# A decode-and-prompt step on one core: two of the next eight weight blocks asked for in front of the SP queue's wait for the samples' vectors

## The chip, the cores and the metric

The kernel runs on one core of one Trainium2 chip. The metric is the device time of one launch in microseconds (us); less is better. The core has five engines, each with its own instruction queue: PE (matmul), ACT (activations and copies out of PSUM), DVE (vector work), POOL, and SP, which here issues nearly all large transfers. A queue runs in order: an instruction that waits for a semaphore holds everything behind it on the same engine. A transfer, once issued, runs by itself and adds 16 to a semaphore when it has landed.

## The reference

Two layers of a hybrid decoder run for a prompt of 256 tokens and for 8 samples of one token each, with shared weights and 1024 channels. All is float32.

```python
xn   = rms_norm(x, ln1_g)
proj = xn @ w_in                    # four mixers' columns, then 4 x 1024 gate columns
y_a, y_b, y_c, y_d = rwkv7(...), hgrn2(...), retention(...), mlstm(...)
gates  = sigmoid(proj[..., o4:]).reshape(B, T, 4, 1024)
branch = einsum('btmw,mwd->btmd', ys, w_branch)
x = x + (sum over m of gates * branch) @ w_out
x = x + peer_ffn(rms_norm(x, ln2_g))      # 16 experts of 16384 for each of 8 heads
```

Each mixer keeps a state of 64 x 64 per head. For the samples that state is read, updated with one token's vectors, and read out again. The states, the last projected row ("shift") and the last rows before a convolution are outputs too.

## The kernel before, in words

Channels lie on the 128 partitions; the 264 columns of a tile are 256 prompt tokens and 8 samples. The two layers are written out one after the other. In a layer come the projections of the mixers (32 column tiles), the mixers, the samples' states, the gates, the branch projection, the output projection, and the experts (the longest part).

**Weight blocks and slots.** The dense weights lie in memory as 44 blocks a layer, each 128 x 2048 floats (1 MB). A block holds two column tiles. `ring` has four slots. `block_of(j, n)` on SP waits until slot j is free (semaphore `w_free[j]`, cleared by `take`), then issues the transfer of block n, which raises `w_full[j]` when it has landed. Blocks 0 to 15 are the mixers' columns, 16 to 31 the gates', 32 to 35 the branches', 36 to 39 the output projection's, 40 to 43 the queries'. PE takes `w_full[j]` before the first of a block's two tiles; ACT (for the gates) signals `w_free[j]` after it has copied the second out of PSUM. The first tile of a block goes to one PSUM bank and the second to another (banks 2 and 3 from tile 14 on), and PE takes `bank_free` of the bank before it writes it; ACT gives it back after its copy.

**Gate tiles as filling.** There are 32 gate tiles, each 8 matmuls of 128 x 264 and one copy by ACT. They depend on nothing but `xn` and their weights, so PE's program puts them between steps of the mixers, in numbers fixed by hand: `EARLY_GATES = 14` of them before the samples' states, then `GATES_AT = (4, 5, 2, 1)` at four places, and the last six before the branches. Gate tile g reads block 16 + g // 2 from slot (g // 2) mod 4. So tiles 14 and 15 read block 23 (slot 3), tiles 16 and 17 block 24 (slot 0), tiles 18 and 19 block 25 (slot 1), 20 and 21 block 26 (slot 2), 22 and 23 block 27 (slot 3).

**The samples' vectors.** PE turns 18 vectors of the samples (L838, L839), ACT copies them out (L1250, L1251, step `act_svt`), SP writes them to a scratch in memory (L452, L453), waits for that, and reads them back in another layout into `gv` and `gvv` (L455, L458). DVE waits for these, then works on the states, L1735 to L1760. Its L1736 raises `dve_sa`; PE sums that over partitions (L844), and DVE needs the sum at L1744. DVE's L1760 raises `dve_po`; PE needs it at L848 and L849, and DVE works on the outcome up to L1773, which PE waits for at L855.

PE's order around this, with the gate tiles (L620) in it:

```python
                gate_tiles(GATES_AT[0])                       # tiles 14 to 17
                close_banks(7)
                e.wait_ge(S("dve_sa"), 1)
                mm(bank(7, HD), C("quads"), sa, start=True, stop=True).then_inc(S("pe_step"), 1)
                gate_tiles(GATES_AT[1])                       # tiles 18 to 22
                e.wait_ge(S("dve_po"), 1)
                ...
                gate_tiles(GATES_AT[2])                       # tiles 23 and 24
                e.wait_ge(S("dve_yy"), 1)
```

ACT, right after its copies for `act_svt`, runs six activations over gates and outputs (L1253 to L1258), and only then copies tiles 14 and 15 out (L1152).

**SP's order before.** Blocks 20 to 23 are issued as their slots come free. Then SP waits for `act_svt`, issues the two writes, waits for them, issues the five reads, waits for `dve_shift` (long raised by then) and issues the output of the shift rows. Then come blocks 24 to 31, in a loop of two rounds of four, and after it the blocks of the branches and of the output projection.

Of the kernel before, what the change touches and what calls it, by code (L numbers as in the profile page):

```python
# [38 lines left out]
N_IN, N_MIXED = 32, 16  # L39
N_BLOCKS = N_IN + 4 + 4 + 4  # L40
# [125 lines left out]
def build(nc, A, O):  # L166

    with ExitStack() as ctx:
# [200 lines left out]
        def S(name):  # L369
            return once[name] if name in once else sems[name]  # L370
# [13 lines left out]
        def step(name):  # L384

            steps = PE_STEPS if name.startswith("pe_") else ACT_STEPS
            return steps.index(name.split("_")[1]) + 1

        def take(e, s, n):

            e.wait_ge(s, n)
            e.sem_clear(s)
# [30 lines left out]
        def _(e):  # L423
            e.dma_start(const[:, 0:FIRST], A["const"][:, 0:FIRST]).then_inc(S("sp_once"), 16)
            e.dma_start(x[:, :, :], A["x"]).then_inc(S("sp_once"), 16)
            for l in range(L):
# [5 lines left out]
                def block_of(j, n):  # L432

                    take(e, w_free[j], 1)
                    e.dma_start(ring[:, j, :], A["w"][bass.ds(n, 1)].rearrange("a p c -> p (a c)")).then_inc(w_full[j], 16)
# [12 lines left out]
                for j in range(4):  # L448
                    block_of(j, l * N_BLOCKS + N_MIXED + 4 + j)

                e.wait_ge(S("act_step"), step("act_svt"))
                e.dma_start(O["scratch"][0:NGLA * NS, :], svt[0:NGLA * NS, :, :].rearrange("p a b -> p (a b)")).then_inc(S("sp_svw"), 16)  # L452
                e.dma_start(O["scratch"][NGLA * NS:NVEC * NS, :], svt2[0:(NVEC - NGLA) * NS, :, :].rearrange("p a b -> p (a b)")).then_inc(S("sp_svw"), 16)  # L453
# [5 lines left out]

                e.wait_ge(S("dve_shift"), 1)  # L460
                e.dma_start(O["shift"][bass.ds(l, 1)].rearrange("a p c -> p (a c)"), out_shift[:, :, :].rearrange("p a b -> p (a b)")).then_inc(S("sp_out"), 16)
                with e.Fori(2, 4) as i:
                    for j in range(4):
                        block_of(j, l * N_BLOCKS + N_MIXED + i * 4 + j)
                for j in range(4):
                    block_of(j, l * N_BLOCKS + N_IN + j)
                for j in range(4):
# [1684 lines left out]
```

## Time and profile before

| | |
|---|---|
| median of 3 runs | 2277.74 us (2268.29 to 2278.77) |
| the profiled execution, its own time | 2278.82 us |
| its span, first to last instruction | 2276.7 us |
| PE busy | 2048.0 us, 90% |
| DVE busy | 1435.7 us, 63% |
| ACT busy | 829.7 us, 36% |
| mean granted TensorE clock | 0.961 |

The profile is one execution. Times are microseconds from the start of its span. PEld is the weight load of a matmul, which overlaps with PE's matmuls. The granted clock is 1.00 at 2.4 GHz and 0.50 at 1.2 GHz; a number between is a stretch in which both occur. In a row of the timeline the bracket at the end is the idle time of the engine before the row, and what ended it; "remote" there means a release that the profile can't name, such as a transfer's landing. Consecutive instructions of one line are merged in one row.

### The profile page before, as it was taken

How to read it: one execution, taken by the hardware profiler on the slowest of the kernel's cores; microseconds unless marked ns; L12 is line 12 of the kernel's file. 1: busy time of each engine (PE TensorE's matmuls, PEld its weight loads, DVE VectorE, ACT ScalarE, POOL GpSimd, SP SyncE). 2: the span in 40 equal slices, each digit the busy share in tenths (PEclk: the TensorE clock that was granted, in tenths of full speed). 3: DMA queues.
4: the chain of work that ended last, by engine and by line, in shares of the span. 5: the costliest groups of instructions: out<-in, count | busy, mean ns of one | idle time of the engine just before them, and what ended most of it. 6: DMA issues, size and time to landing. Idle time of an engine off the chain costs nothing.

```text
span 2276.7 us, 37176 instructions
## 1 busy us (share of the span) xinstructions
PE 2048.0 (90%) x13044; PEld 1253.7 (55%) x13044; DVE 1435.7 (63%) x3297; ACT 829.7 (36%) x2404; POOL 753.9 (33%) x658
## 2 busy tenths in 40 slices
PE   6999989989999777999889898899899997789996
PEld 5777768764444222555477776787544442235553
DVE  1425464559999898544623454754699989974445
ACT  1221222034445675333322213220444457743333
POOL 0400000025545567444403000000354557754452
PEclk9999889999999999999989999999999999999998
DMA  6330233559999999999853201434799999999996
GB/s 254 122 113 2 78 123 128 186 176 384 375 366 400 367 384 374 369 382 398 345 213 111 94 21 61 156 132 165 259 365 384 386 361 348 375 367 393 378 361 246
DMA packets 120670, 597.81 MB, mean 263 GB/s; under 512 B 38635, under 2 KB 40587, under 8 KB 57227
## 3 DMA queue, kind: packets, MB, share of 16 engines
q0 software_dynamic: 76032, 417.87, 47.4%
q1 hardware_dynamic: 42784, 174.46, 21.1%
q10 hardware_dynamic: 1696, 3.45, 0.4%
q8 instruction: 89, 1.46, 0.3%
q14 instruction: 69, 0.57, 0.1%
HBM read 724.97 MB, written 6.58 MB: 321 GB/s over the span
## 4 chain that ended last, share of the span: by engine, by line
PE 57%; DVE 18%; DMA 12%; issue 7%; ACT 3%; POOL 1%; another core or an unknown queue 1%; SPq 0%; DVEq 0%; POOLq 0%; ACTq 0%
PE ps L945 11%; PE ps L1012 11%; PE ps L557 10%; DMA arena<-in_uv,arena 7%; PE ps L620 7%; DMA ring<-in_uv,arena 4%; DVE arena L1933 4%; PE ps L971 3%; PE ps L908 3%; PE ps L877 3%; PE ps L891 3%; DVE arena L1835 1%; DVE arena L1834 1%; DVE arena L1831 1%
## 5 line engine op out<-in xcount | busy, mean ns | idle before, releaser
L1416 POOL DMA_INDIRECT arena<-in_uv,arena x264 | 340.1, 1288 | 298.9 <-PE ps L945 250.7
L1416 POOL DMA_INDIRECT ring<-in_uv,arena x264 | 328.8, 1246 | 290.2 <-PE ps L945 251.4
L1933 DVE SCALAR_TENSOR_TENSOR arena<-ring,arena 128x1024 bf16<-128x1024 f32 x264 | 320.4, 1225 | 134.5 <-DMA ring<-in_uv,arena 124.1
L1933 DVE SCALAR_TENSOR_TENSOR arena<-arena 128x1024 bf16<-128x1024 f32 x264 | 320.9, 1225 | 128.1 <-DMA arena<-in_uv,arena 117.3
L945 PE MATMUL ps<-arena 64*64 64x512 f32 x2112 | 295.5, 631 | 67.1 <-ACT arena L1309 66.9
L945 PE MATMUL ps<-ring,arena 64*64 64x512 f32 x2112 | 293.2, 630 | 56.0 <-ACT arena L1309 53.9
L1307 ACT ACTIVATE arena<-arena 128x1 f32<-128x1 f32 x528 | 106.5, 202 | 574.7 <-DVE arena L1933 573.8
L1406 POOL COPY arena<-arena 128x8 uint32 (+1 forms) x66 | 34.6, 525 | 740.7 <-DVEq L1907 740.3
L971 PEld LDWEIGHTS ps<-xn,ub 128*128 128x128 f32 x1024 | 181.5, 192 | 176.3 <-issue 159.1
L971 PE MATMUL ps<-xn,ub 128*128 128x256 f32 x1024 | 277.4, 404 | 0.0
L1012 PE MATMUL ps<-hold,ub 128*128 128x256 f32 x1024 | 265.8, 398 | 0.0
L1012 PEld LDWEIGHTS ps<-hold,ub 128*128 128x128 f32 x1024 | 182.7, 191 | 150.6 <-issue 132.0
L620 PE MATMUL ps<-xn,ring 128*128 128x264 f32 x1024 | 245.1, 398 | 14.5 <-remote 12.1
L557 PE MATMUL ps<-xn,ring 128*128 128x264 f32 x1024 | 241.1, 396 | 14.5 <-ACTq L1100 10.5
L557 PEld LDWEIGHTS ps<-xn,ring 128*128 128x128 f32 x1024 | 199.4, 196 | 54.1 <-issue 15.7
L620 PEld LDWEIGHTS ps<-xn,ring 128*128 128x128 f32 x1024 | 197.4, 195 | 51.7 <-issue 17.0
L1309 ACT ACTIVATE arena<-const,arena 128x64 f32<-128x64 f32 x528 | 184.3, 349 | 17.2
L1308 ACT ACTIVATE arena<-arena 128x1 f32<-128x1 f32 x528 | 155.6, 295 | 17.2
L945 PEld LDWEIGHTS ps<-arena 64*64 64x64 f32 x2112 | 56.4, 133 | 164.1 <-issue 164.1
L945 PEld LDWEIGHTS ps<-ring,arena 64*64 64x64 f32 x2112 | 57.4, 134 | 141.2 <-issue 140.9
L1105 ACT ACTIVATE arena<-ps 128x264 f32<-128x264 f32 x64 | 25.2, 394 | 233.8 <-PE ps L557 233.7
L1152 ACT ACTIVATE arena<-ps 128x264 f32<-128x264 f32 x50 | 19.3, 389 | 201.7 <-PE ps L620 201.3
(427 smaller groups left out, 2264.7 us busy)
## 6 DMA issues: line engine op xcount, KB each, us to landing
ring<-in_w SPq DMA_DIRECT2D x88, 1024.0 KB, 4.9
ub<-in_ud SPq DMA_DIRECT2D x64, 512.0 KB, 7.6
ub<-in_uv SPq DMA_DIRECT2D x64, 512.0 KB, 7.7
ring<-in_uv,arena POOLq DMA_INDIRECT x264, 11.0
arena<-in_uv,arena POOLq DMA_INDIRECT x264, 11.6
hold<-in_st SPq DMA_DIRECT2D x2, 2048.0 KB
out_st<-hold SPq DMA_DIRECT2D x2, 2048.0 KB
const<-in_const ACTq DMA_DIRECT2D x1, 2723.0 KB, 13.5
```

The costliest lines, as they stand in the source:

```text
L557: m = mm(bank(b), ring[:, j, at:at + P], xn[:, kt, :], start=kt == 0, stop=kt == KT - 1)
L620: m = mm(bank(b), ring[:, j, at:at + P], xn[:, kt, :], start=kt == 0, stop=kt == KT - 1)
L877: m = mm(bank(b), ring[:, j, at:at + P], yy[:, 2 * m_ + k, :], start=k == 0, stop=k == 1)
L891: m = mm(bank(6 + o % 2), ring[:, j, at:at + P], src[:, kt, :], start=kt == 0, stop=kt == KT - 1)
L945: m = mm(ps[chunk(q ^ half), SUM_BANK[tt] + half, :], dg[chunk(q), k, :], row(k)[chunk(q), D + 512 * half:D + 512 * half + 512], start=Fal ...
L971: m = mm(bank(4 + j % 4, SEQ), ub[:, j % UB, kt * P:kt * P + P], xn[:, kt, 0:SEQ], start=kt == 0, stop=kt == KT - 1)
L1012: m = mm(bank(4 + dt // 2, SEQ, SEQ * (dt % 2)), ub[:, j % UB, dt * P:dt * P + P], hd[:, j, :], start=False, stop=False, skip_group_check= ...
L1307: own(act(hge[:, k:k + 1], hid[:, k:k + 1], ACT.Gelu))
L1308: own(act(hgg[:, k:k + 1], hge[:, k:k + 1], ACT.Copy, scale=gate))
L1309: act(dg[:, k, :], C("channel"), ACT.Copy, scale=hgg[:, k:k + 1]).then_inc(dg_full[k], 1)
L1416: e.indirect_dma_start(out=row(k), out_offset=None, in_=A["uv"], in_offset=bass.IndirectOffsetOnAxis(ap=ix[:, par, k:k + 1], axis=0), **sk ...
L1933: stt(prod[:, n % 2, :], u, 1.0, xtok[:, tt, :], ALU.mult, ALU.mult, accum_out=hid[:, k:k + 1]).then_inc(S("dve_hid"), 1)
```

## The change

Blocks 24 and 25 are asked for in front of SP's wait for `act_svt`, right behind block 23. Blocks 26 to 31 stay behind the output of the shift rows, and are written out one by one in place of the loop. The slots are the same as before, and so is the order of the blocks among themselves. Nothing changes on PE, ACT, DVE or POOL.

```diff
                 for j in range(4):
                     block_of(j, l * N_BLOCKS + N_MIXED + 4 + j)
 
+                for j in range(2):
+                    block_of(j, l * N_BLOCKS + N_MIXED + 8 + j)
                 e.wait_ge(S("act_step"), step("act_svt"))
...
                 e.wait_ge(S("dve_shift"), 1)
                 e.dma_start(O["shift"][bass.ds(l, 1)].rearrange("a p c -> p (a c)"), out_shift[:, :, :].rearrange("p a b -> p (a b)")).then_inc(S("sp_out"), 16)
-                with e.Fori(2, 4) as i:
-                    for j in range(4):
-                        block_of(j, l * N_BLOCKS + N_MIXED + i * 4 + j)
+                for n in range(2, 8):
+                    block_of(n % 4, l * N_BLOCKS + N_MIXED + 8 + n)
```

## Rows read from the trace of the kernel before

**Rows 1.** The page: its first line, and busy time, share and instructions by engine.

```profile
span 2276.7 us, 37176 instructions
PE 2048.0 (90%) x13044; PEld 1253.7 (55%) x13044; DVE 1435.7 (63%) x3297; ACT 829.7 (36%) x2404; POOL 753.9 (33%) x658
```

**Rows 2.** Windows by stage: layer 0's mixers and projections, layer 0's experts.

```profile
core 0: us, PE busy (x) PEld busy (x) DVE busy (x) ACT busy (x) POOL busy (x), PEclk, DMA share, GB/s
0.00:442.00 442.00, 393.66 (x2510) 322.44 (x2510) 191.59 (x411) 91.69 (x183) 25.24 (x34) 0.95 0.34 122
442.00:1140.00 698.00, 630.16 (x3994) 303.23 (x3994) 522.29 (x1232) 322.16 (x1017) 347.04 (x297) 0.97 0.92 357
```

**Rows 3.** Timeline of SP, layer 0, 225 to 400 us: issues of transfers.

```profile
start us, us, engine line op out<-in xcount [idle before <-releaser]
234.62 26.60 SPq L435 DMA_DIRECT2D ring<-in_w  x4
...
302.42 1.38 SPq L453 DMA_DIRECT2D scratch<-arena  x1
...
309.71 89.92 SPq L435 DMA_DIRECT2D ring<-in_w  x14
```

**Rows 4.** Timeline of ACT: tiles 9, 11, 14 and 15 in layer 0; 14 and 15 in layer 1.

```profile
269.61 0.37 ACT L1152 ACTIVATE hold<-ps 128x264 f32<-128x264 f32 x1
...
275.02 0.39 ACT L1152 ACTIVATE hold<-ps 128x264 f32<-128x264 f32 x1 [3.17 <-PE ps L620]
...
309.71 0.65 ACT L1152 ACTIVATE arena<-ps 128x264 f32<-128x264 f32 x2
...
1433.17 0.65 ACT L1152 ACTIVATE arena<-ps 128x264 f32<-128x264 f32 x2
```

**Rows 5.** Timeline of PE and DVE around the samples' states, layer 0.

```profile
301.17 7.29 PE L620 MATMUL ps<-xn,ring 128*128 128x264 f32 x32
...
311.46 1.87 DVE L1736 TENSOR_REDUCE arena<-arena 128x64 f32<-128x1024 f32 x1
...
315.10 10.24 PE L620 MATMUL ps<-xn,ring 128*128 128x264 f32 x32 [6.64 <-remote]
...
321.16 3.36 DVE L1742 TENSOR_TENSOR hold<-hold,arena 128x3072 f32<-128x3072 f32 x1
...
325.35 18.02 PE L620 MATMUL ps<-xn,ring 128*128 128x264 f32 x80
...
325.63 0.23 DVE L1744 TENSOR_SCALAR arena<-ps 128x64 f32<-128x64 f32 x1 [1.10 <-PE ps L844]
...
343.93 1.08 PE L848 MATMUL ps<-const,arena 128*128 128x32 f32 x8 [0.56 <-DVE arena L1760]
...
345.06 7.37 PE L620 MATMUL ps<-xn,ring 128*128 128x264 f32 x32
...
351.05 0.71 DVE L1773 TENSOR_TENSOR arena<-arena 128x528 f32<-128x528 f32 x1
...
352.27 1.94 PE L855 MATMUL ps<-arena,const 128*128 128x264 f32 x8
```

**Rows 6.** The same place in layer 1: timeline of PE and DVE.

```profile
1437.39 8.89 PE L620 MATMUL ps<-xn,ring 128*128 128x264 f32 x32 [5.48 <-remote]
...
1447.06 0.23 DVE L1744 TENSOR_SCALAR arena<-ps 128x64 f32<-128x64 f32 x1
...
1465.35 1.08 PE L848 MATMUL ps<-const,arena 128*128 128x32 f32 x8 [1.03 <-DVE arena L1760]
```

**Rows 7.** Windows, for the granted clock (the column before the last two).

```profile
308.50:315.10 6.60, 0.00 (x0) 0.00 (x1) 4.87 (x4) 1.86 (x5) 0.00 (x0) 0.66 0.72 247
...
318.00:321.00 3.00, 3.00 (x9) 2.28 (x8) 3.00 (x3) 0.00 (x0) 0.00 (x0) 0.52 1.01 429
321.00:325.30 4.30, 4.30 (x22) 3.69 (x21) 3.49 (x2) 0.39 (x1) 0.00 (x0) 1.00 0.09 38
...
1436.00:1440.00 4.00, 2.60 (x6) 2.08 (x7) 4.00 (x2) 0.00 (x0) 0.00 (x0) 0.63 1.01 424
1440.00:1444.00 4.00, 4.00 (x18) 3.37 (x18) 3.96 (x5) 0.39 (x1) 0.00 (x0) 0.94 0.95 401
```

**Rows 8.** The weight blocks' transfers (line 435), layer 0, issue to landing.

```profile
DMA to landing us min/median/max: 4.7/5.0/9.3
```

## The prediction

> **What bounds the kernel now.** The page comes first: PE is busy for 90% of the span [rows 1], so one looks for what PE waits for. The windows by stage show that the change lies in the smaller part: a layer's projections and mixers end near 442 us, and the experts take 698 us more with no block of the ring in them [rows 2]. What the change can do, it does at one place in each layer, around 308 us and around 1432 us. There the chain of waits matters more than any busy share, and the timelines give it.
>
> In layer 0 PE starts gate tiles 14 and 15 at 301.17 and is done 7.29 us later. Then it idles for 6.64 us, until 315.10, when block 24 has landed [rows 5]; SP had issued it only at 309.71, behind the samples' vectors and the shift rows [rows 3]. In layer 1 the same idle time is 5.48 us, up to 1437.39 [rows 6]. These 12.1 us of an idle PE are what the change goes for. The second reading is whether the end waits for them. It hardly does. DVE works on the states at the same time, and PE's next step of use to DVE is the sum at L844. In layer 0 DVE stood idle for that sum by 1.10 us before L1744; in layer 1 its L1744 has no wait at all [rows 5, 6]. Further on the roles are reversed: after tiles 18 to 22 PE waits for DVE's L1760, by 0.56 us in layer 0 and 1.03 us in layer 1, before L848 [rows 5, 6]. So from 310 to 344 us DVE's chain of states sets the pace, and PE has only filling to do beside it.
>
> **The change, part by part.** *The two early blocks.* The issue of block 24 needs slot 0, which ACT frees after tile 9: its copy starts at 269.61 and takes 0.37 us, so block 24 goes out near 270. Block 25 needs slot 1, freed after tile 11, at 275.02 + 0.39 = 275.4 [rows 4]. With the slowest landing seen, 9.3 us [rows 8], both have landed by 285. SP stands at these two waits in place of the wait for `act_svt`, which ends just before the write at 302.42 [rows 3]; so nothing queued behind them comes later, with 26 us to spare. They land more than 15 us before the small transfers of the vectors begin, so they can't be in their way. Cost: nothing.
>
> *What then holds tile 16.* Not the block, but PSUM. Tile 16 goes to the bank of tile 14, and ACT copies tiles 14 and 15 out only at 309.71, the first of the two taking 0.39 us [rows 4]. So tile 16 starts near 310.1 in place of 315.10, and PE still idles for 310.1 − 308.46 = 1.6 us. In layer 1 it starts at 1433.17 + 0.39 = 1433.6 in place of 1437.39. The gain in PE's start is 5.0 us and 3.8 us, not 6.64 and 5.48.
>
> *The clock in that stretch.* From 308.5 to 315.1 the mean granted clock is 0.66, so it fell to 1.2 GHz for (1 − 0.66) × 2 × 6.6 = 4.5 us, from 310.6 on. It is still 0.52 from 318 to 321, and 1.00 after that [rows 7]: it rose about 5.8 us after PE began again. This made tiles 16 and 17 take 10.24 us in place of the 7.2 us that two tiles take at 2.4 GHz (18.02 us for five) [rows 5]: 3.0 us. In layer 1 the tiles took 8.89 us, 1.7 us too long [rows 6], with the clock up again at about 1440.5, 3.1 us after the start [rows 7]. With an idle time of 1.6 us the clock may stay up: in layer 1 it fell only 5.1 us into the idle time, in layer 0 already 2.1 us in. If it falls all the same, there is room: tiles 16 and 17 end at 317.3, or at 320.4 with 3.0 us more, `dve_sa` has been there since 313.3 (the end of L1736), and DVE wants the sum only when L1742 ends, at 324.5 [rows 5]. What is gained is therefore DVE's wait, 325.63 − 324.52 = 1.1 us, in layer 0, and nothing in layer 1.
>
> *What comes late next.* With the sum at 317.5, tiles 18 to 22 take their 18.0 us and end at 335.5. Their blocks are there: 25 since 285; 26 is issued at 309.7, right behind the shift rows, and with 9.3 us lands at 319.0, while tile 20 starts at 317.5 + 7.2 = 324.7; 27 goes out when tile 15 has been copied, at 310.4, and has until tile 22, at 331.9. Then PE waits for L1760, whose end moves from 343.9 to 342.8. The idle time that stood ahead of tile 16 now stands ahead of L848: 342.8 − 335.5 = 7.3 us, where it was 0.56. In layer 1 the tiles end at 1433.6 + 7.2 + 0.2 + 18.0 = 1459.0, and L848 stays at 1465.35: 6.3 us, where it was 1.03. These are as long as the two idle times that brought the clock to 1.2 GHz in the trace (6.64 and 5.48 us).
>
> *What that costs.* Ahead of tile 16 a slow clock was nearly covered by DVE. Behind L848 it is not. PE there does L848 and L849 (about 1.1 us) and tiles 23 and 24 (7.37 us), and begins L855 at 352.27, while DVE's L1773 is ready at 351.76 [rows 5]. PE is the later one by half a microsecond, so each microsecond that PE loses there moves L855 and all that follows: tile 25, L863, the last six tiles and the branches, which PE works through without a break worth naming. The rows bound the loss: 1.7 us (layer 1's tiles 16 and 17) and 3.0 us (layer 0's), and 0 if the clock stayed up. Both slowed stretches followed idle times like the new ones, and the work is as long as theirs, so I take their mean, 2.35 us, in each layer.
>
> *The loop written out.* SP loses a few register instructions between issues. It waits for free slots there, so this is worth nothing. One thing has no firm price: the issue at L453 took 1.38 us in layer 0 [rows 3] without a wait that the trace shows, and it is on the path to DVE's start. Where the instructions of SP lie may change such a delay; I bound it by 1 us either way.
>
> **The sum.** Layer 0: −1.1 + 2.35 = +1.25 us. Layer 1: 0 + 2.35. Together +3.6 us; with the bounds of the clock term from 2 × 1.7 − 1.1 = +2.3 to 2 × 3.0 − 1.1 = +4.9. Made against the profiled execution, the span goes from 2276.7 to 2280.3, and its own time from 2278.82 to 2282.4; that execution is 1.1 us above the median, so I predict 2281.3 for the median. The three runs differ by 10.5 us, from 2268.29 to 2278.77. So 0.5%, or 11.4 us, is about what a measurement of this kernel can tell from no change, and the forecast is well within it.
>
> A rule that speaks the other way is in the Trainium skill, TensorE: Matmul & The Clock Gate, section "HAM oscillation — how this bites in real kernels": waits for transfers between bursts of matmuls let the clock fall again and again, and order the work so that PE stays warm. By that rule, with this trace's durations, the change would give back the 3.0 and 1.7 us that the slow clock took; the rows on L1760 say that the idle time is moved and not removed, so the sum goes by them.
>
> **The rivals.** *A. No price of the clock (0.12).* If the clock came back before it mattered, or did not fall, the change is worth −1.1 us: 2276.6. For it: in layer 1 the clock held 5.1 us into an idle time, so a fall is not sure after 6.3 us. Against it: both long idle times in this place brought the clock down.
>
> *B. The whole wait comes off (0.05).* PE's idle time of 6.64 + 5.48 us and the 3.0 + 1.7 us of slow clock go from the end: 16.8 us, so 2260.9, faster by 0.7%. This holds if PE's order, and not DVE's chain, sets the pace up to L848. Against it are the two waits of PE for L1760 and the missing wait before layer 1's L1744. The Trainium skill, Perfetto Trace Analysis, section "Optimization Strategy", tells one to find an engine's gaps and make what they wait for start sooner; by that alone one would expect this. The waits say that the next thing is late at once.
>
> *C. Slower by more than 0.5% (0.06).* The slow clock lasts past L848 to the branches. PE has nine more tiles there in each layer, at 3.6 us each 32 us, all on the path. It decides from a low clock of (11.4 + 1.1) × 2 / 2 = 12.5 us in each layer; at 14 us in each the time is 2277.7 − 1.1 + 14 = 2290.6. Against it: after both restarts seen, the clock was up within 5.8 us.
>
> *D. The blocks still come late (0.03).* If slots 0 and 1 came free only after the vectors' step, nothing would change: 2277.7. The copies at 269.61 and 275.02 exclude it but for a mistake in the reading.
>
> **How the numbers follow.** The forecast, a small loss of 2.3 to 4.9 us lost in the spread of the runs, has 0.74. Its own range takes the spread of the runs below it: from 2269 to 2288. A and D lie within this; B and C lie outside with 0.11. Sides by more than 0.5%: faster 0.06 (B, and a chance draw of fast executions), slower 0.08 (C, and a draw on the other side, since the forecast is already above), within 0.86.
>
> **What the profile after would show.** Block 24's issue near 270 and block 25's near 275; tile 16 at about 310.1 with an idle time of 1.6 us that ends with ACT's copy, not a landing; no wait of DVE before L1744; L848 at about 342.8 and 1465.3 with 7.3 and 6.3 us of idle PE ahead of it; the clock at 0.5 at that place, and tiles 23 and 24 with 8.8 to 10.2 us in place of 7.37; L877 later by 1 to 3 us in each layer, counted from the landing of the vectors. The prediction is wrong if the clock is up behind L848, if L877 comes sooner by more than 1.1 us, or if the experts' part changes by more than its executions differ.

## The result, and the profile after

The changed kernel takes 2280.62 us (median of 15 runs, 2269.73 to 2285.31) where the kernel before takes 2272.85 (15 runs, 2268.29 to 2278.77). The ratio is 1.0027, with a 95% interval of 1.0015 to 1.0039: 3 to 9 us slower, inside the 0.5% that was called no change. The prediction was 2281.3, made as +3.6 us on a kernel before of 2277.7. That it lies only 0.7 us off is luck: the median of three runs that it started from was 4.9 us above the median of 15, and the step that it added was smaller than the 6.1 us that the ratio stands for. Run again beside other kernels the changed one gave 1.0016 (0.9996 to 1.0036).

The spans of single executions differ by more than the effect, so the reading goes by a section that the change can touch: from DVE's first instruction on the states (L1735 before) to the first product of the branches (L877 before). In the changed kernel all lines behind SP's part are one higher: L620 is L621, L1735 is L1736, L877 is L878. A product of the program stands in the rows as two records, so that two gate tiles of 8 products are x32.

| us | before | after | difference |
|---|---|---|---|
| layer 0: first on the states to the branches | 310.20 to 384.00: 73.80 | 307.41 to 382.30: 74.89 | +1.1 |
| layer 1 | 1432.70 to 1505.41: 72.71 | 1435.69 to 1511.35: 75.66 | +2.95 |

The first fence is the timeline of the kernel before at these four points, the second the page of the changed kernel.

```profile
310.20 1.23 DVE L1735 TENSOR_TENSOR arena<-hold,arena 128x1024 f32<-128x1024 f32 x1 [20.05 <-DMA arena<-scratch]
...
384.00 6.27 PE L877 MATMUL ps<-arena,ring 128*128 128x264 f32 x27 [1.00 <-remote]
...
1432.70 1.23 DVE L1735 TENSOR_TENSOR arena<-hold,arena 128x1024 f32<-128x1024 f32 x1 [19.13 <-DMA arena<-scratch]
...
1505.41 4.93 PE L877 MATMUL ps<-arena,ring 128*128 128x264 f32 x21 [1.00 <-remote]
```

```profile
span 2278.5 us, 37128 instructions
PE 2050.5 (90%) x13044; PEld 1255.1 (55%) x13044; DVE 1434.5 (63%) x3297; ACT 830.2 (36%) x2404; POOL 746.4 (33%) x658
```

PE, DVE and ACT run the same number of instructions as before, for the same time within 3 us. The timeline of the changed kernel in layer 0, from the issue of blocks 24 and 25 on:

```profile
265.10 7.45 SPq L435 DMA_DIRECT2D ring<-in_w  x2
...
306.64 0.65 ACT L1153 ACTIVATE arena<-ps 128x264 f32<-128x264 f32 x2
307.16 7.38 PE L621 MATMUL ps<-xn,ring 128*128 128x264 f32 x32 [1.78 <-ACT arena L1153]
307.41 1.23 DVE L1736 TENSOR_TENSOR arena<-hold,arena 128x1024 f32<-128x1024 f32 x1 [20.18 <-DMA arena<-scratch]
...
321.81 0.23 DVE L1745 TENSOR_SCALAR arena<-ps 128x64 f32<-128x64 f32 x1
...
339.90 1.92 PE L849 MATMUL ps<-const,arena 128*128 128x32 f32 x8 [7.33 <-DVE arena L1761]
341.63 0.61 PE L850 MATMUL ps<-const,arena 128*128 128x32 f32 x2
342.05 8.68 PE L621 MATMUL ps<-xn,ring 128*128 128x264 f32 x32
...
348.06 0.71 DVE L1774 TENSOR_TENSOR arena<-arena 128x528 f32<-128x528 f32 x1
...
350.57 1.94 PE L856 MATMUL ps<-arena,const 128*128 128x264 f32 x8
...
382.30 4.04 PE L878 MATMUL ps<-arena,ring 128*128 128x264 f32 x17 [1.00 <-remote]
```

Tiles 16 and 17 start right after ACT's first copy, with 1.78 us of idle PE where there were 6.64 [rows 4, 5]. They run at the full clock, 7.38 us in place of 10.24, and DVE's L1745 has no wait. Then comes the other side: PE is idle for 7.33 us ahead of L849, where it was 0.56 [rows 5]. L849 takes 1.92 us in place of 1.08, tiles 23 and 24 take 8.68 in place of 7.37, and L856 starts 1.8 us after the end of L1774: PE is now clearly the late one. From there to the branches both kernels take 31.7 us. In layer 1 the same:

```profile
1435.69 1.23 DVE L1736 TENSOR_TENSOR arena<-hold,arena 128x1024 f32<-128x1024 f32 x1 [18.91 <-DMA arena<-scratch]
1436.64 7.38 PE L621 MATMUL ps<-xn,ring 128*128 128x264 f32 x32 [1.78 <-ACT arena L1153]
...
1468.21 1.91 PE L849 MATMUL ps<-const,arena 128*128 128x32 f32 x8 [6.16 <-DVE arena L1761]
...
1470.36 9.42 PE L621 MATMUL ps<-xn,ring 128*128 128x264 f32 x32
1479.62 1.94 PE L856 MATMUL ps<-arena,const 128*128 128x264 f32 x8
...
1511.35 8.94 PE L878 MATMUL ps<-arena,ring 128*128 128x264 f32 x39 [1.00 <-remote]
```

The windows of the changed kernel show why. The clock, in the third column from the end, is 0.51 and 0.50 in the first and third stretch, which are the end of the idle time and the first work after it; in the kernel before the slow stretches lay around tiles 16 and 17 [rows 7].

```profile
337.90:344.80 6.90, 4.90 (x17) 4.34 (x18) 4.31 (x11) 0.00 (x0) 0.00 (x0) 0.51 0.00 0
344.80:352.00 7.20, 7.20 (x34) 6.16 (x33) 3.93 (x2) 0.78 (x2) 0.00 (x0) 1.00 0.40 146
...
1464.30:1474.60 10.30, 6.39 (x20) 5.47 (x21) 7.71 (x13) 0.00 (x0) 0.00 (x0) 0.50 0.00 0
1474.60:1480.00 5.40, 5.40 (x26) 4.62 (x25) 2.43 (x2) 0.49 (x2) 0.00 (x0) 1.00 0.47 146
```

What the slow stretch costs can be read directly. From the start of L848 to the start of L855 the kernel before takes 8.34 us in both layers; from L849 to L856 the changed kernel takes 10.67 and 11.41 us. That is 2.33 and 3.07 us more.

### The profile page after: what moved, and what is told of

Same layout as the page of the kernel before. It is cut to its first block and busy times, and to the rows that moved or that the text cites. A ratio compares the mean times of both kernels' runs of the same rounds, so it can differ in the third digit from the quotient of the medians.

```text
span 2278.5 us, 37128 instructions
## 1 busy us (share of the span) xinstructions
PE 2050.5 (90%) x13044; PEld 1255.1 (55%) x13044; DVE 1434.5 (63%) x3297; ACT 830.2 (36%) x2404; POOL 746.4 (33%) x658
## 5 line engine op out<-in xcount | busy, mean ns | idle before, releaser
L1417 POOL DMA_INDIRECT ring<-in_uv,arena x264 | 339.3, 1285 | 286.5 <-PE ps L946 240.3
L1417 POOL DMA_INDIRECT arena<-in_uv,arena x264 | 326.2, 1236 | 308.4 <-PE ps L946 262.7
L621 PE MATMUL ps<-xn,ring 128*128 128x264 f32 x1024 | 248.0, 401 | 5.7 <-ACT arena L1153 3.6
L621 PEld LDWEIGHTS ps<-xn,ring 128*128 128x128 f32 x1024 | 199.4, 197 | 44.2 <-issue 8.5
```

Of the source, the lines that this page charges most:

```text
L621: m = mm(bank(b), ring[:, j, at:at + P], xn[:, kt, :], start=kt == 0, stop=kt == KT - 1)
L1417: e.indirect_dma_start(out=row(k), out_offset=None, in_=A["uv"], in_offset=bass.IndirectOffsetOnAxis(ap=ix[:, par, k:k + 1], axis=0), **sk ...
```

## The experiments

Each kernel was timed beside the kernel before on the same chip, with 6 to 15 executions of each new kernel. Theory 1 is that of the prediction: the wait is moved to a place where the slow clock behind it is not covered. "Sections" are the two stretches of the table above, read from each kernel's own trace, which is one execution. Two pairs tell how well they repeat: the changed kernel's two traces differ by 0.15 us at most, and those of the kernel before and of the one with only the loop written out by 0.6 us in layer 0.

| kernel | ratio to before (95%) | sections, layers 0 and 1, us |
|---|---|---|
| before | 1 | 73.80, 72.71 |
| changed, first trace | 1.0027 (1.0015 to 1.0039) | 74.89, 75.66 |
| changed, second trace | 1.0016 (0.9996 to 1.0036) | 75.04, 75.63 |
| loop written out alone | 1.0008 (0.9990 to 1.0026) | 73.20, 72.71 |
| products of no use in the wait | 0.9991 (0.9972 to 1.0010) | 74.38, 72.71 |
| seven tiles ahead of L848, blocks early | 0.9937 (0.9916 to 0.9959) | 65.67, 66.31 |
| the same, blocks late | 0.9986 (0.9967 to 1.0006) | 73.04, 71.43 |
| one block early | 1.0030 (1.0010 to 1.0049) | 75.28, 75.55 |
| three blocks early | 1.0065 (1.0040 to 1.0090) | 75.08, 76.37 |
| four blocks early | 1.0100 (1.0074 to 1.0125) | 75.52, 75.53 |
| seven tiles, ACT's copy earlier | 0.9932 (0.9908 to 0.9956) | 67.24, 65.73 |
| seven tiles, one block early | 0.9935 (0.9910 to 0.9960) | 65.60, 66.13 |

**The loop alone.** Half of the change: blocks 24 to 31 written out, all behind the shift rows.

```diff
-                with e.Fori(2, 4) as i:
-                    for j in range(4):
-                        block_of(j, l * N_BLOCKS + N_MIXED + i * 4 + j)
+                for n in range(0, 8):
+                    block_of(n % 4, l * N_BLOCKS + N_MIXED + 8 + n)
```

> Only the loop over blocks 24 to 31 is written out; no block is asked for earlier. Theory 1 (all of the change's cost lies in PE's idle time moved ahead of L848 and in the slow clock behind it): like the kernel before, within 2 us, about 2273. Theory 2 (SP's instructions lie elsewhere, and that costs or shifts something): about as slow as the changed kernel, +6 to +8 us, near 2280.

2274.77 us against 2274.88, and sections as in the kernel before (layer 0's is 0.6 us shorter; DVE waited 0.58 us there for the sum where it was 1.10). By the sections Theory 2 falls; the interval alone, which ends at +5.9 us, only just leaves out the +6 that it asked for.

**Products of no use in the wait.** On the changed kernel; nothing is left out, 13 products are added.

```diff
                 gate_tiles(GATES_AT[1])
+                for _ in range(13):
+                    mm(bank(6), C("ones"), xn[:, 0, :], start=True, stop=True)
                 e.wait_ge(S("dve_po"), 1)
```

> The changed kernel with 13 products of no use (ones times one tile of xn, into a bank that nothing reads then) between tile 22 and the wait for dve_po, 5.8 us of the 7.3 and 6.2 us in which PE idled. Theory 1: the clock stays at 1.00 behind L848, tiles 23 and 24 take 7.4 us in place of 8.7 and 9.4, and the section from DVE's first instruction on the states to L878 gets shorter by 2.1 us in layer 0 and 3.0 in layer 1: 5 us below the changed kernel, about 2275, and 1 us below the kernel before by this part alone. Theory 2 (the loss lies elsewhere): no change against the changed kernel, 2280.

2273.56 us against 2274.88. Layer 1 did what Theory 1 says: with 0.52 us of idle time left, tiles 23 and 24 take 7.37 us and the section is 72.71, 2.95 below the changed kernel and equal to the kernel before. More work for PE made the layer faster than in the changed kernel. Layer 0 gave back only 0.5 us of the 2.1 expected. There 1.72 us of idle time were left, and the clock fell after all: the timeline of this kernel (behind the added products its lines are two higher than in the changed kernel), and two windows of it.

```profile
335.91 5.95 PE L848 MATMUL ps<-xn,const 128*128 128x264 f32 x26
343.58 1.08 PE L851 MATMUL ps<-const,arena 128*128 128x32 f32 x8 [1.72 <-DVE arena L1763]
...
344.74 9.03 PE L621 MATMUL ps<-xn,ring 128*128 128x264 f32 x32
...
1465.25 1.08 PE L851 MATMUL ps<-const,arena 128*128 128x32 f32 x8 [0.52 <-DVE arena L1763]
...
1466.39 7.37 PE L621 MATMUL ps<-xn,ring 128*128 128x264 f32 x32
```

```profile
341.00:344.00 3.00, 1.28 (x8) 0.80 (x6) 2.49 (x4) 0.00 (x0) 0.00 (x0) 1.00 0.00 0
344.00:348.00 4.00, 4.00 (x16) 3.28 (x16) 2.92 (x9) 0.00 (x0) 0.00 (x0) 0.59 0.00 0
```

**Seven tiles ahead of L848.** If the idle time is only moved, work has to be moved into it. Two tiles go from the last group of six to the place ahead of L848.

```diff
-GATES_AT = (4, 5, 2, 1)
+GATES_AT = (4, 7, 2, 1)
```

> The changed kernel with two more gate tiles ahead of L848 (7 in place of 5) and two fewer in the last group (4 in place of 6). Theory 1: the 7.3 and 6.2 us of idle PE take 7.1 us of work that was on the path at the end; in layer 0 8 to 9 us less than the kernel before, in layer 1 6 to 7 less (the tiles run over the wait for L1760 by about 1 us there): 14 to 15 us below the kernel before, near 2258. If the last group is the cover of DVE's work up to dve_yn (it ends 11 us after the start of that group, four tiles take 14.2), a loss of up to 3 us of that would show as a wait ahead of L878. Theory 2 (idle time there is not the matter): no gain.

2259.87 us against 2274.88: the version that beats both. The sections are 8.1 and 6.4 us shorter than before, 14.5 in all, and the ratio of 0.9937 is 14.3 us. L849 starts without a wait and the clock stays at 1.00. Timeline of this kernel, layer 0:

```profile
319.70 25.14 PE L621 MATMUL ps<-xn,ring 128*128 128x264 f32 x112
344.82 1.08 PE L849 MATMUL ps<-const,arena 128*128 128x32 f32 x8
...
362.36 14.40 PE L621 MATMUL ps<-xn,ring 128*128 128x264 f32 x64
377.81 2.49 PE L878 MATMUL ps<-arena,ring 128*128 128x264 f32 x10 [1.04 <-remote]
```

DVE is ready for the branches 3.1 us before the last four tiles end, so their cover was not needed at six.

**The same move with the blocks late.** The edit of `GATES_AT` on the kernel before.

> The same two tiles moved, but on the kernel before, where blocks 24 and 25 come late. Theory 1: PE is late at L848 by the two tiles, 7.1 us, less the idle time that it had there (0.6 and 1.0 us), and gets the 7.1 us back in the last group: about 1.6 us faster than before in all, 2271. Rival: with the blocks late the same move is worth as much as with them early (-14 us).

2271.00 against 2274.88, sections 0.8 and 1.3 us shorter, as Theory 1 says. So by the sections the blocks early alone are worth +4 us, the tiles moved alone −2, both −14.5. The early blocks spare PE 8.6 us of idle time (6.64 + 5.48 − 2 × 1.78) and 4.4 us of slow clock (10.24 + 8.89 − 2 × 7.38) around tiles 16 and 17, and that is worth something only with work to put there. With the two tiles moved in both kernels, the early blocks make the sections 7.4 and 5.1 us shorter, 12.5 in all, nearly all of these 13.

**Other numbers of early blocks.** In the change, `range(2)` becomes 1, 3 or 4, and the second loop starts there. First the changed kernel once more, on the chip of these three.

> The changed kernel once more, beside the other places for the blocks. By the two sections, from DVE's first instruction on the states to the branches' first product, it is 1.1 us longer in layer 0 and 3.0 us in layer 1 than the kernel before, 4 us in all. Theory 1 expects a ratio near 1.0018, about 2279, and Theory 3 (a further cost outside these sections) near 1.0034.

1.0016, and sections 1.2 and 2.9 us longer than before, as in the first trace. The interval holds both of the expected ratios, so the timing doesn't decide on Theory 3.

> Only block 24 in front of the wait; 25 to 31 behind the shift rows. Block 25 is then issued at about 309.7 and lands by 315 to 319, while tile 18 wants it at 317.5. Theory 1: PE is idle ahead of L848 all the same (5 to 7 us) and the clock falls; like the changed kernel, +4 us against the kernel before. Rival (the second early block is what costs): like the kernel before.

One early block does all that two do: 6.93 and 6.02 us of idle PE ahead of L849 and the sections of the changed kernel. The rival falls.

> Block 26 too in front of the wait. Its slot is freed by the copy of tile 13, near 300.1, 2 us ahead of act_svt. Its 1 MB then moves while the vectors are written and read back. Theory 1 alone: like the changed kernel, +4 us. Rival (transfers of weights get in the way of the vectors): DVE's start on the states comes later against act_svt by up to 5 us a layer, the time in which the block lands, so up to +14 us.

Its ratio is 1.0065. PE's section is like the changed kernel's (a little longer in layer 1), but the vectors come late. From ACT's second copy (L1251 before) to DVE's first instruction it takes 11.9 us in layer 0 (8.6 before) and 9.8 in layer 1 (7.6 before). Timeline of SP and DVE in this kernel, layer 0:

```profile
296.06 0.33 SPq L435 DMA_DIRECT2D ring<-in_w  x1
...
298.39 0.59 SPq L455 DMA_DIRECT2D scratch<-arena  x1
304.25 0.39 SPq L457 DMA_DIRECT2D arena<-scratch  x1
...
309.55 1.23 DVE L1736 TENSOR_TENSOR arena<-hold,arena 128x1024 f32<-128x1024 f32 x1 [23.19 <-DMA arena<-scratch]
```

Block 26 goes out 2 us before the vectors' writes, and SP waits 5.9 us from the second write to the first read; in the kernel before that is 2.6 us in layer 0, of which the issue at L453 itself took 1.38 [rows 3]. In layer 1 it is 3.8 us in place of 1.7. The extra 3.4 and 2.2 us of the vectors and the 1.3 and 3.7 us of the sections make 10.5 us; the interval allows 9 to 20.

> All four blocks in front of the wait. Block 27 needs slot 3, which ACT frees only with the copy of tile 15, 310.4 in the kernel before, 8.4 us behind act_svt. SP stands there with the vectors' writes behind it: DVE starts on the states 8.4 us later in each layer, or up to 13 with the block's own transfer in the way, and PE idles by as much more. +21 to +30 us against the kernel before, near 2296 to 2305. If SP's queue were not what the vectors wait for, it would stay at +4.

Its ratio is 1.0100. Block 27 needs the slot that ACT gives back at tile 15, and SP stands at it with the vectors' writes behind it:

```profile
302.75 8.93 SPq L435 DMA_DIRECT2D ring<-in_w  x2
311.74 0.42 SPq L454 DMA_DIRECT2D scratch<-arena  x1
312.21 0.42 SPq L455 DMA_DIRECT2D scratch<-arena  x1
316.87 0.39 SPq L457 DMA_DIRECT2D arena<-scratch  x1
```

ACT's second copy begins at 304.32, the write waits until 311.74, and DVE starts at 322.13: 17.8 us for what took 8.6, and 17.8 in place of 7.6 in layer 1. With the sections (+1.7 and +2.8) that is 24 us; 17 to 28 were measured. SP's stand at the slot is the larger part of it. The rest is the transfer of block 27, issued just ahead of the writes: from the second write to the first read it takes 4.7 us here, 2.6 before. So in this kernel two is the most that can stand ahead of the wait at no cost to the vectors. Three fail by the transfer in the way, four by the queue and the transfer together.

**Two refinements of the seven tiles.** In the first, ACT copies tile 14 out between its activations, which takes away the 1.78 us ahead of tile 16. In the second, block 24 alone is early.

```diff
                 act(proj[:, RT + 6:RT + 8, :], proj[:, RT + 6:RT + 8, :], ACT.Silu)
+                gate_tiles(1)
...
-                gate_tiles(sum(GATES_AT[:3]))
+                gate_tiles(sum(GATES_AT[:3]) - 1)
```

> The kernel with seven tiles ahead of L848 (fill), and ACT copies tile 14 out after the second of its six activations and not after the sixth. Tile 16 then starts right behind tile 15, and the 1.8 us in which PE waited for the copy go. In layer 1 the seven tiles ran past L1760's end by 1.1 us, which this takes away; in layer 0 there was no overrun above 0.2 us. So 1 us less than fill, which 5 rounds can hardly tell: 2258 to 2260, and the trace decides: no idle time ahead of tile 16, and L848 in layer 1 right at the end of L1760.

0.9932, not to be told from 0.9937. In layer 1 the section is 0.6 us shorter, half of what was expected, since PE then waits 1.04 us for DVE ahead of L849. In layer 0, where no loss was expected, it is 1.6 us longer: 2.48 us of idle time stand ahead of L849 now, and the clock fell. It is the change's own lesson again, in small. Timeline and a window of this kernel:

```profile
338.99 1.08 PE L849 MATMUL ps<-const,arena 128*128 128x32 f32 x8 [2.48 <-DVE arena L1762]
```

```profile
339.00:343.00 4.00, 4.00 (x17) 3.39 (x18) 2.55 (x9) 0.00 (x0) 0.00 (x0) 0.66 0.00 0
```

> Fill with block 24 alone in front of the wait. Block 25 lands by 319 at the latest and tile 18 wants it at 317.5. If one early block is enough: as fill, -14 us against the kernel before. If tile 18 waits for its block, up to 2 us a layer are lost again: -10 us.

0.9935 and the sections of the kernel with two early blocks: one is enough, and tile 18 does not wait.

## Why the prediction was right

**The early blocks cost nothing on SP.** Right: issued at 265.1 and 272.2, and the vectors take 8.8 and 7.6 us from ACT's copy to DVE's start, as before (8.6 and 7.6). A detail was off: block 24 went out at 265.1, 1.6 us before ACT's copy of tile 9 began at 266.70, so the slot is given back without waiting for that copy. In the program the signal is an instruction of its own behind the copy; that ACT's queue passes it while the copy is still to run is the likely reading, which no run tests.

**PSUM, and not the block, holds tile 16.** Right: 1.78 us, ended by ACT's copy, in both layers (1.6 predicted).

**DVE's wait goes, 1.1 us in layer 0 and nothing in layer 1.** Right, by the missing wait before L1745 in both layers.

**The idle time moves ahead of L848.** Right in place and size: 7.33 and 6.16 us for 7.3 and 6.3. Counted from the start of the span, L849 came 2.9 us earlier (layer 0) and later (layer 1) than forecast, because all before it was that much earlier or later; counted from DVE's start it is as forecast.

**The clock's price behind it, 1.7 to 3.0 us a layer, 2.35 taken.** Right in layer 0 and just above the upper bound in layer 1: 2.33 and 3.07 us from L849 to L856, 5.4 where 4.7 were taken. Part of it lies ahead of the tiles, from which the forecast took its size: L849 takes 0.84 us more, and tiles 23 and 24 alone take 8.68 and 9.42 us, the first just under the 8.8 to 10.2 that was forecast. With DVE's 1.1 us the sections' sum was +4.0 for +3.6. The products of no use showed the slow clock as the cause in layer 1: with PE kept busy, all 2.95 us came back. In layer 0 the clock fell all the same, so there the cause rests on the windows and the durations.

**The rivals.** A (no price) and C (slow up to the branches) are excluded by the windows, B (faster by 16.8 us) and D (no earlier block) by the timeline. B is worth a second look. Of its 16.8 us PSUM keeps 3.6 (1.78 in each layer), and of the 13 us left 12.5 can be had, but only with the two tiles moved. Without them the wait for a block was not what the end waited for.

**What stays open.** The first ratio stands for 6.1 us with an interval from 3.4 to 8.9, the second for 3.6; the sections account for 4.0 to 4.2. The rest, if there is one, was not found: the executions of one kernel differ by some 20 us, and outside the two sections the two traces differ by 2 us in favour of the changed kernel.

## What to carry to other kernels

A wait that is long on one engine is worth what the chain through the other engines lets it be. Before you take it away, ask what the engine waits for next, and whether it then stands in a place where a slow clock is covered. When a stall has moved, move work after it: here the two halves gave +4 and −2 us, and together −14.5. An issue can be put ahead of a wait on the same queue only if its own condition is sure to come first and its bytes are through before the small transfers behind the wait.

## What the runs showed of the hardware that was not expected

A short idle time of PE can be followed by the slow clock too. Ahead of L848 (L849 or L851 in the other kernels), idle times of 0.5 to 1.04 us left the clock at 1.00. 1.72 us (layer 0 of the kernel with the added products) and 2.48 us (layer 0 with ACT's copy earlier) were each followed by a stretch at 1.2 GHz that made tiles 23 and 24 take 1.7 us more. It began when PE was at work again, 1.1 and 1.3 us after the start of the small products. Ahead of tile 16, 1.78 us left the clock at 1.00 in all 16 cases (eight traces, two layers), but other work surrounds it there, so whether the length, the place or the moment decides is not shown.

That the moment has a part is seen in the long idle times, where the two layers run the same instructions. The clock fell 2.1 us into the one of layer 0 and 5.1 us into that of layer 1 in the kernel before, and 5.3 and 2.2 us into them in the changed kernel. The Trainium skill, TensorE: Matmul & The Clock Gate, section "What's actually happening", says that the chip watches activity in windows that are free-running and do not reset when a kernel starts. The different moments of the fall agree with that; no run here shows such a window itself.

One transfer of 1 MB, issued 2 us ahead of two writes of 144 KB together, made the vectors late by 3.4 and 2.2 us (layers 0 and 1 of the kernel with three early blocks).
